# Hybrid decoder step on one core: the attention probabilities are scaled by their sums on the vector engine, head by head, in place of GpSimd

## The chip, the cores and the metric

The kernel runs on 1 core of one Trainium2 chip. The metric is the device time of one execution in microseconds (us); the lower the better. A core has five engines that run their own instruction streams and meet at semaphores: TensorE (PE: matmuls and transposes into the PSUM memory), VectorE (DVE), ScalarE (ACT), GpSimd (POOL) and SyncE (SP, which here only starts DMAs). The profile names a TensorE weight load PEld, and an engine's queue instructions (semaphores, drains, DMA issues) by a q behind its name.

## The reference

Four layers, each `x <- x + RMSNorm_post(mixer(RMSNorm_pre(x)))`, on 1024 prompt tokens and 8 sample tokens, which share all weights. Layer 0 and 3 are gated MLPs, layer 2 is a gated linear recurrence, and layer 1, the one that the change touches, is attention over a sliding window of 128 keys, with a sink value for each of its 16 heads:

```python
def sink_softmax(scores, mask, sinks):
    s = jnp.where(mask, scores.astype(jnp.float32), -jnp.inf)
    sink = sinks.astype(jnp.float32)[..., None, None]
    m = jnp.maximum(jnp.max(s, axis=-1, keepdims=True), sink)
    e = jnp.exp(s - m)
    return e / (jnp.sum(e, axis=-1, keepdims=True) + jnp.exp(sink - m))
...
    o = jnp.einsum('bnkgqs,bnskd->bnqkgd', p.astype(vv.dtype), vv).reshape(bsz, t_len, N_HEADS * HEAD_DIM)
    out = (o * jax.nn.silu(g)) @ w_out
```

What is changed is the division by the sum, for the prompt tokens: the exponentials `e` are multiplied by the reciprocal of their sum.

## The kernel before, in words

Everything is fp32. A matrix product is made of three matmul passes on parts of the operands (high x high, low x high, high x low); the high part of a weight tile is made by ACT (`w_high`, L992), the low part by DVE (`w_low`, L1434), and each weight tile is loaded by SP into a ring of three places. Activations lie with features on the 128 partitions and 1032 tokens along the free dimension, worked on in three parts of 344 columns.

In the attention layer (`layer_b` on each engine) the prompt is cut into 8 blocks of 128 queries, and the 16 heads into 4 groups of 4. That makes 32 steps (`STEPS`), and in step `i` an engine does its part for several steps at once. The chain of one step is

- PE `scores(i)` (L816): queries by keys into PSUM, 4 heads x 256 keys;
- DVE `maxima(i)` (L1773): scale, mask and row maximum, from PSUM to the SBUF tile `sc` (one of two buffers, `i % 2`), 4 operations; it ends with signal `B`;
- ACT `exps(i)` (L1278): the exponentials in place in `sc`, with their sums, 4 operations; ends with signal `X`;
- DVE `sums(i)` (L1784, L1786): sum plus sink, and reciprocal, into `rq`; signal `Rq`;
- POOL `normals` (L527): one operation multiplies `sc`, 128 rows x 4 heads x 256, by `rq`; signal `C`;
- PE `turns(i)` (L830): transposes `sc` (16 of them) into PSUM; signal `TP`;
- ACT `copies(i)` (L1287): PSUM to `pt`; signal `PC`;
- PE `values(i)` (L844): the product with the values; signal `PV`;
- DVE `outputs(i)` (L1794), ACT `highs(i)` (L1294), DVE `lows(i)` (L1800): gate, and split into high and low for the output product.

The order on each engine is written out by hand. In its iteration `i` DVE does `maxima(i + 1)`, then the readings of projection pieces (`read_piece`, L1752 and L1749), `outputs(i - 1)`, `lows(i - 2)`, then `sums(i + 1)`, and behind it what the step brings: `gate_silu` (L1762), `w_low` and `rotate_q` (the rotary turn of a query tile: L1700, L1701, L1703; six times in the steps, the first three earlier) and the pieces of attention for the sample tokens (`sample_keys` L1806 to L1815, `sample_maxima` L1820 to L1828, `sample_normals` L1833 to L1842, `sample_probs`). ACT does `copies(i - 1)`, `exps(i + 1)`, `highs(i - 1)`, and behind them DMA issues of `swap` (L1228, which feeds the rotary turn), `w_high` and `gate_tanh` (L1272). PE does pieces of the query and gate projections (`piece`, L798, 24 matmuls each), `values(i - 1)`, `scores(i + 2)` and `turns(i)`; from step 27 on, pieces of the output product (`out_part`, L855) stand in the place of the projections. `maxima(i + 1)` waits for `scores(i + 1)` and for `turns(i - 1)`, which frees its buffer.

The lines of the attention loop on DVE are these:

```python
for i in range(STEPS):
    if i + 1 < STEPS:
        maxima(i + 1)
    ...
    if i + 1 < STEPS:
        sums(i + 1)
    for p in late_end(i - 1) if i else ():
        gate_silu(p)
    ...
    for j in units_ended(i - 1) if i else []:
        w_low(L.u0 + j + 2)
        ...
            rotate_q(m)
```

Of the kernel before, what the change touches and what calls it, by code (L numbers as in the profile page):

```python
# [17 lines left out]
ALU = mybir.AluOpType  # L18
# [3 lines left out]
P = 128  # L22
# [11 lines left out]
WIN = 128  # L34
# [51 lines left out]
def build(nc, io):  # L86
    with ExitStack() as ctx:
# [76 lines left out]
        for i, kind in enumerate("abca"):  # L164
            L = Layer()
# [49 lines left out]
            if kind == "b":  # L215
# [9 lines left out]
                o = X_AT  # L225
# [37 lines left out]
            if kind == "c":  # L263
# [23 lines left out]
                o = X_AT  # L287
# [85 lines left out]
        STEPS = 4 * NBLK  # L373
# [13 lines left out]
        def pieces_ended(entries):  # L387

            return [p for p, _, end in entries if end == KT]
# [130 lines left out]
        @block.gpsimd  # L520
        def _(pool):

            def normals(L):

                for i in range(STEPS):
                    pool.wait_ge(*L.Rq.at(i + 1))
                    nc.gpsimd.tensor_tensor(L.sc[:, i % 2], L.sc[:, i % 2],  # L527
                                            L.rq[:, i % 2].rearrange("p (h o) -> p h o", o=1).to_broadcast([P, 4, 2 * WIN]),
                                            ALU.mult).then_inc(L.C.sem, 1)

            def gate_input(L, m):

                pool.wait_ge(*L.sig.at(m + 1))
                nc.gpsimd.tensor_tensor(L.it[:, m % 2, :], L.it[:, m % 2, :], L.xc[:, m, :], ALU.mult).then_inc(L.ix.sem, 1)

            LA, LB, LC, LZ = layers
            normals(LB)
            for m in range(KT):
                gate_input(LC, m)

# [880 lines left out]
        def _(dve):  # L1421
            V = nc.vector
# [269 lines left out]
            def layer_b(L):  # L1692
# [88 lines left out]
                def sums(i):  # L1781
                    p = i % 2
                    dve.wait_ge(*L.X.at(i + 1))
                    V.tensor_tensor(L.rq[:, p], L.mx[:, p, 2, :], L.mx[:, p, 3, :], ALU.add)  # L1784
                    V.drain()
                    V.reciprocal(L.rq[:, p], L.rq[:, p]).then_inc(L.Rq.sem, 1)  # L1786

                def outputs(i):
                    qd, n = divmod(i, NBLK)
# [76 lines left out]
                dve.wait_ge(*L.at_in.at(16 * 5))  # L1866
                maxima(0)
                sums(0)
                to_rotate = []
                for i in range(STEPS):  # L1870
# [11 lines left out]
                    if i + 1 < STEPS:  # L1882
                        sums(i + 1)
# [294 lines left out]
```

## Time and profile before

| | before |
|---|---|
| median of 3 runs | 2393.58 us (2392.2 to 2395.04) |
| the profiled execution | 2394.26 us, its span 2392.1 us |
| PE busy | 2320.3 us, 97% of the span |
| DVE busy | 1232.4 us, 52% |
| ACT busy | 889.1 us, 37% |
| POOL busy | 90.7 us, 4% |
| granted TensorE clock, mean | 0.99 of full |
| the attention steps | about 885 to 1145 us of the span |
| PE busy in the attention steps | 241.47 of 260 us |
| DVE, ACT, POOL busy there | 172.47, 138.84, 70.46 us |

Times in rows are microseconds from the start of the span, unless a column says ns. Busy shares tell little by themselves: what counts is which engine the others wait for, stretch by stretch.

### The profile page before, as it was taken

What the parts mean: (1) busy time and instruction counts of PE and PEld (TensorE: products, weight loads), DVE (VectorE), ACT (ScalarE), POOL (GpSimd) and SP (SyncE); (2) the same over time, 40 slices, a digit from 0 to 9 for tenths busy, and PEclk for the clock granted to TensorE, in tenths of its full rate; (3) what the DMA queues carried; (4) which work ended last, traced back from release to release, by engine and by line L of the source; (5) the groups of instructions that cost most, each with busy time, mean ns of one, the idle gap of its engine ahead of it and who ended that gap; (6) DMA issues with size and microseconds to landing.
All of it is one profiled execution on the core that took longest, in us unless ns stands there. A gap on an engine that the chain in (4) does not pass through costs nothing.

```text
span 2392.1 us, 36016 instructions
## 1 busy us (share of the span) xinstructions
PE 2320.3 (97%) x15487; PEld 2236.2 (93%) x15487; DVE 1232.4 (52%) x1759; ACT 889.1 (37%) x1280; POOL 90.7 (4%) x44
## 2 busy tenths in 40 slices
PE   8999999999999899998999999999999999999997
PEld 7999999999999798877989999979999999999996
DVE  4444445454433756667267888274444544545235
ACT  5323332332332534556352366363223332333221
POOL 0000000000000002222000010000000000000000
PEclk9999999999999999999999999999999999999998
DMA  4111111111121331111322111322111111111213
GB/s 137 45 45 45 45 45 38 43 45 45 36 98 45 127 111 54 45 45 37 107 83 70 45 45 45 118 84 77 45 54 36 45 45 38 43 45 45 89 46 107
DMA packets 58494, 145.86 MB, mean 61 GB/s; under 512 B 8904, under 2 KB 29528, under 8 KB 58328
## 3 DMA queue, kind: packets, MB, share of 16 engines
q1 hardware_dynamic: 53056, 135.34, 17.5%
q10 hardware_dynamic: 5280, 8.22, 1.3%
q8 instruction: 122, 2.00, 0.4%
q14 instruction: 36, 0.29, 0.0%
HBM read 121.47 MB, written 18.37 MB: 58 GB/s over the span
## 4 chain that ended last, share of the span: by engine, by line
PE 82%; DVE 9%; ACT 3%; DVEq 3%; ACTq 1%; issue 1%; DMA 1%; SPq 0%
PE ps L552 62%; PE ps L576 7%; PE ps L798 4%; PE ps L710 2%; PE ps L634 2%; DVE x L1476 1%; DVE l_acc L1473 1%; PE ps L816 1%; DVE w_lo L1434 1%; PE ps L855 1%; PE ps L844 1%; PE ps L703 1%; DVE l_sc L1773 1%; ACT l_h_hi L1043 1%; DVE l_hs L1988 1%
## 5 line engine op out<-in xcount | busy, mean ns | idle before, releaser
L552 PE MATMUL ps<-l_h_hi,w_hi 128*128 128x344 f32 x2448 | 527.1, 324 | 5.6 <-DVE w_lo L1434 5.6
L552 PE MATMUL ps<-l_h_lo,w_hi 128*128 128x344 f32 x2448 | 520.4, 321 | 0.0
L552 PE MATMUL ps<-l_h_hi,w_lo 128*128 128x344 f32 x2448 | 516.6, 319 | 0.0
L552 PEld LDWEIGHTS ps<-l_h_hi,w_hi 128*128 128x128 f32 x2448 | 409.2, 188 | 10.1 <-DVE w_lo L1434 6.8
L552 PEld LDWEIGHTS ps<-l_h_lo,w_hi 128*128 128x128 f32 x2448 | 414.7, 189 | 0.0
L552 PEld LDWEIGHTS ps<-l_h_hi,w_lo 128*128 128x128 f32 x2448 | 408.2, 188 | 0.0
L1434 DVE TENSOR_TENSOR w_lo<-w_raw,w_hi 128x1024 fp32r<-128x1024 f32 x182 | 227.7, 1252 | 250.3 <-ACT w_hi L992 240.2
L992 ACT ACTIVATE w_hi<-w_raw 128x1024 fp32r<-128x1024 f32 x182 | 190.8, 1049 | 109.9 <-DMA w_raw<-in_wu 78.9
L1551 DVE TENSOR_TENSOR l_tmp<-ps,rx 128x1032 f32<-128x1032 f32 x64 | 78.9, 1233 | 285.5 <-PE ps L552 285.3
L552 PE MATMUL ps<-l_y_lo,w_hi 128*128 128x344 f32 x816 | 173.1, 320 | 0.0
L552 PE MATMUL ps<-l_y_hi,w_hi 128*128 128x344 f32 x726 | 154.7, 321 | 0.8 <-DVEq L2002 0.8
L552 PE MATMUL ps<-l_y_hi,w_lo 128*128 128x344 f32 x726 | 153.1, 319 | 0.0
L1137 ACT ACTIVATE l_tmp<-l_tmp 128x1032 f32<-128x1032 f32 x32 | 34.2, 1067 | 303.9 <-DVEq L1592 303.9
L552 PEld LDWEIGHTS ps<-l_y_lo,w_hi 128*128 128x128 f32 x816 | 137.9, 189 | 0.0
L552 PEld LDWEIGHTS ps<-l_y_hi,w_hi 128*128 128x128 f32 x726 | 121.6, 188 | 1.7 <-DVEq L2002 1.1
L552 PEld LDWEIGHTS ps<-l_y_hi,w_lo 128*128 128x128 f32 x726 | 120.9, 188 | 0.0
L1142 ACT ACTIVATE l_tmp<-l_tmp 128x1032 f32<-128x1032 f32 x32 | 34.2, 1068 | 226.6 <-DVEq L1597 226.5
L1121 ACT ACTIVATE l_v<-l_v 128x1032 f32<-128x1032 f32 x32 | 34.1, 1067 | 214.9 <-DVEq L1573 214.9
L527 POOL TENSOR_TENSOR l_sc<-l_sc,l_rq 128x1024 f32<-128x1024 f32 x32 | 70.5, 2202 | 1072.6 <-DVE l_rq L1786 1072.6
L798 PE MATMUL ps<-l_h_hi,w_hi 128*128 128x344 f32 x288 | 97.1, 337 | 0.0
L1551 DVE TENSOR_TENSOR l_v<-ps,rx 128x1032 f32<-128x1032 f32 x28 | 34.5, 1233 | 120.2 <-PE ps L552 118.1
L1278 ACT ACTIVATE l_sc<-l_sc,l_mx 128x256 f32<-128x256 f32 x128 | 63.5, 497 | 82.3 <-DVEq L1779 82.3
(248 smaller groups left out, 3617.5 us busy)
## 6 DMA issues: line engine op xcount, KB each, us to landing
w_raw<-in_wu SPq DMA_DIRECT2D x182, 512.0 KB, 3.5
x_save<-x SPq DMA_DIRECT2D x9, 1376.0 KB, 5.8
x<-x_save SPq DMA_DIRECT2D x21, 516.0 KB, 7.1
l_sw<-l_q ACTq DMA_DIRECT2D x32, 129.0 KB, 2.8
out_y<-x SPq DMA_DIRECT2D x6, 688.0 KB, 3.5
x<-in_xt SPq DMA_DIRECT2D x4, 688.0 KB, 10.7
x<-in_xt SPq DMA_DIRECT2D x5, 516.0 KB, 6.7
x<-in_xt ACTq DMA_DIRECT2D x3, 516.0 KB, 3.6
```

The source lines that it names most:

```text
L527: nc.gpsimd.tensor_tensor(L.sc[:, i % 2], L.sc[:, i % 2], L.rq[:, i % 2].rearrange("p (h o) -> p h o", o=1).to_broadcast([P, 4, 2 * WIN]), ...
L552: mm = nc.tensor.matmul(ps[:, 3 * slot + ch, 0:CW], wt[:, w, k, :], mv[:, k, ch * CW:(ch + 1) * CW], start=(k == 0 and t == 0), stop=(k == ...
L576: mm = nc.tensor.matmul(ps[:, 3 * slot + ch, 0:CW], wt[:, u % W_RING, k, :], mv[:, k, part(ch)], start=(k == 0 and t == 0), stop=(k == KT ...
L634: mm = nc.tensor.matmul(ps[:, 3 * j + c, 0:CW], wt[:, (u + j) % W_RING, k, :], mv[:, k, part(c)], start=(k == 0 and t == 0), stop=(k == KT ...
L710: mm = nc.tensor.matmul(ps[:, 6 + b // 4, (b % 4) * P:(b % 4 + 1) * P], vt[:, b, :], L.ws[:, g, :], start=True, stop=True)
L798: mm = nc.tensor.matmul(ps[:, p % 2, 0:CW], wt[:, w % W_RING, k, :], mv[:, k, part(ch)], start=(k == 0 and t == 0), stop=(k == KT - 1 and ...
L992: nc.scalar.activation(w_hi[:, u % W_RING], w_raw[:, u % W_RING], ACT.Copy).then_inc(w_hi_done, 1)
L1137: nc.scalar.activation(L.tmp[:, 0, :], L.tmp[:, 0, :], ACT.Gelu_apprx_tanh).then_inc(L.u_act.sem, 1)
L1142: nc.scalar.activation(L.tmp[:, 1, :], L.tmp[:, 1, :], ACT.Silu).then_inc(L.g_act.sem, 1)
L1278: nc.scalar.activation(L.sc[:, p, h, :], L.sc[:, p, h, :], ACT.Exp, bias=L.mx[:, p, 1, h:h + 1], accum_out=L.mx[:, p, 2, h:h + 1])
L1434: V.tensor_tensor(w_lo[:, u % W_RING], w_raw[:, u % W_RING], w_hi[:, u % W_RING], ALU.subtract).then_inc(w_lo_done, 1)
L1551: V.tensor_tensor(chunks(out), psum_result(slot), chunks(rx[:]), ALU.mult)
```

## The change

The 32 POOL multiplications of `sc` go, with the signal `Rq`. In their place DVE, directly behind the reciprocal, drains and does four `tensor_scalar` operations, one for each head (128 rows x 256 columns, SBUF to SBUF in place, the factor a column of `rq`); the last one gives signal `C`. PE, ACT and SP do what they did. POOL keeps the 8 multiplications of `gate_input` in layer 2.

```diff
         @block.gpsimd
         def _(pool):
-            def normals(L):
-
-                for i in range(STEPS):
-                    pool.wait_ge(*L.Rq.at(i + 1))
-                    nc.gpsimd.tensor_tensor(L.sc[:, i % 2], L.sc[:, i % 2],
-                                            L.rq[:, i % 2].rearrange("p (h o) -> p h o", o=1).to_broadcast([P, 4, 2 * WIN]),
-                                            ALU.mult).then_inc(L.C.sem, 1)
...
             LA, LB, LC, LZ = layers
-            normals(LB)
...
                     V.tensor_tensor(L.rq[:, p], L.mx[:, p, 2, :], L.mx[:, p, 3, :], ALU.add)
                     V.drain()
-                    V.reciprocal(L.rq[:, p], L.rq[:, p]).then_inc(L.Rq.sem, 1)
+                    V.reciprocal(L.rq[:, p], L.rq[:, p])
+                    V.drain()
+                    for h in range(4):
+                        mult = V.tensor_scalar(L.sc[:, p, h, :], L.sc[:, p, h, :], L.rq[:, p, h:h + 1], None, ALU.mult)
+                    mult.then_inc(L.C.sem, 1)
```

Nine lines go ahead of it, so a DVE line of before stands 9 lower in the changed kernel up to the reciprocal (L1786 is L1777 there), and 5 lower behind it (L1794 is L1789).

On DVE the first rotary turn inside the steps stands, before, in this order behind the sums of step 2 (w_lo is the low part of a weight tile, the next three rows are `rotate_q`, ISA rows are the first of the maxima):

```order
L1784 TENSOR_TENSOR l_rq<-l_mx 128x4
L1786 RECIPROCAL l_rq<-l_rq 128x4
L1434 TENSOR_TENSOR w_lo<-w_raw,w_hi 128x1024
L1700 TENSOR_TENSOR l_sw<-l_sw,l_sin 128x1032
L1701 TENSOR_TENSOR l_q<-l_q,l_cos 128x1032
L1703 TENSOR_TENSOR l_q<-l_q,l_sw 128x1032
L1773 ISA l_sc,l_mx<-ps,l_mask,l_sink 128x256
```

The same place in the changed kernel:

```order
L1775 TENSOR_TENSOR l_rq<-l_mx 128x4
L1777 RECIPROCAL l_rq<-l_rq 128x4
L1780 TENSOR_SCALAR l_sc<-l_sc,l_rq 128x256 x4
L1425 TENSOR_TENSOR w_lo<-w_raw,w_hi 128x1024
L1691 TENSOR_TENSOR l_sw<-l_sw,l_sin 128x1032
L1692 TENSOR_TENSOR l_q<-l_q,l_cos 128x1032
L1694 TENSOR_TENSOR l_q<-l_q,l_sw 128x1032
L1764 ISA l_sc,l_mx<-ps,l_mask,l_sink 128x256
```

The four multiplications stand ahead of the weight's low part, of the rotary turn, and of the maxima of the next step. Near the end of the steps, in DVE's iterations 28 and 29, there is nothing but `sample_probs` between a reciprocal and the next maxima. Before, the first of the two:

```order
L1786 RECIPROCAL l_rq<-l_rq 128x4
L1849 COPY l_pts<-ps 128x256
L1850 TENSOR_TENSOR l_zo<-ps,l_dx 8x128
L1773 ISA l_sc,l_mx<-ps,l_mask,l_sink 128x256
L1773 ISA l_mx 128x1
```

And in the changed kernel:

```order
L1777 RECIPROCAL l_rq<-l_rq 128x4
L1780 TENSOR_SCALAR l_sc<-l_sc,l_rq 128x256 x4
L1844 COPY l_pts<-ps 128x256
L1845 TENSOR_TENSOR l_zo<-ps,l_dx 8x128
L1764 ISA l_sc,l_mx<-ps,l_mask,l_sink 128x256
```

Here too the multiplications come between the reciprocal and the next maxima.

## Rows read from the trace of the kernel before

**Rows 1.** Whom PE waited for from 885 to 1147 us: total, times, longest

```profile
PE ps L844 <- ACT l_pt L1287: 10.5, 7, 3.2
PE ps L816 <- DVEq L1779: 7.9, 4, 2.8
```

**Rows 2.** Timeline of PE in the steps: start, duration; in brackets the idle before

```profile
901.14 1.08 PE L844 MATMUL ps<-l_pt,l_vtok 128*64 128x256 f32 x8 [1.50 <-ACT l_pt L1287]
...
912.38 1.13 PE L816 MATMUL ps<-l_kd,l_q 64*128 64x256 f32 x8 [1.53 <-DVEq L1779]
...
1059.13 1.14 PE L816 MATMUL ps<-l_kd,l_q 64*128 64x256 f32 x8 [1.92 <-DVEq L1779]
...
1066.05 1.98 PE L844 MATMUL ps<-l_pt,l_vtok 128*64 128x256 f32 x8 [3.20 <-ACT l_pt L1287]
...
1091.18 1.14 PE L816 MATMUL ps<-l_kd,l_q 64*128 64x256 f32 x8 [2.81 <-DVEq L1779]
...
1120.99 2.08 PE L816 MATMUL ps<-l_kd,l_q 64*128 64x256 f32 x8 [1.67 <-DVEq L1779]
...
1141.66 1.08 PE L844 MATMUL ps<-l_pt,l_vtok 128*64 128x256 f32 x8 [2.61 <-ACT l_pt L1287]
```

**Rows 3.** The POOL multiplication: ns min/median/max, first and last start

```profile
L527 POOL TENSOR_TENSOR l_sc<-l_sc,l_rq x32: 1894/1897/2788, 892.0 to 1140.7; 128x1024 f32<-128x1024 f32 x32
```

**Rows 4.** Timelines of DVE and POOL at the first rotary turn; L1700 as a group

```profile
903.53 1.19 DVE L1434 TENSOR_TENSOR w_lo<-w_raw,w_hi 128x1024 fp32r<-128x1024 f32 x1
904.64 2.92 DVE L1700 TENSOR_TENSOR l_sw<-l_sw,l_sin 128x1032 f32<-128x1032 f32 x1
...
903.69 2.79 POOL L527 TENSOR_TENSOR l_sc<-l_sc,l_rq 128x1024 f32<-128x1024 f32 x1 [4.51 <-DVE l_rq L1786]
...
L1700 DVE TENSOR_TENSOR l_sw<-l_sw,l_sin x9: 1170/2924/2926, 850.2 to 1070.2; 128x1032 f32<-128x1032 f32 x9
```

**Rows 5.** DVE tensor_scalar elsewhere: L1961 and L1962 with two factors, L1777 with constants

```profile
L1961 DVE TENSOR_SCALAR l_xc<-l_xr,cvec x8: 803/806/809, 1278.6 to 1358.0; 128x1024 f32<-128x1024 f32 x8
...
L1962 DVE TENSOR_SCALAR l_xc<-l_st,cvec x8: 281/284/289, 1279.3 to 1358.7; 128x8 f32<-128x8 f32 x8
...
L1777 DVE TENSOR_SCALAR l_mx<-l_mx x32: 169/170/255, 889.0 to 1137.7; 128x4 f32<-128x4 f32 x32
```

**Rows 6.** Other DVE operations in the steps of which some took longer

```profile
L1762 DVE SCALAR_TENSOR_TENSOR l_gate<-l_th,l_gate x6: 484/486/2032, 1085.2 to 1123.5; 128x344 f32<-128x344 f32 x6
...
L1810 DVE COPY l_qz<-l_q x4: 183/185/1593, 1094.2 to 1096.2; 64x32 f32<-64x32 f32 x4
...
L1824 DVE TENSOR_TENSOR l_sm<-l_sm,l_sk x1: 674/674/674, 1109.3 to 1109.3; 128x2 f32<-128x2 f32 x1
...
L1835 DVE TENSOR_TENSOR l_sm<-l_sm x1: 793/793/793, 1116.9 to 1116.9; 128x2 f32<-128x2 f32 x1
```

**Rows 7.** Timelines of ACT and DVE in the last steps

```profile
1105.16 0.51 ACT L1278 ACTIVATE l_sc<-l_sc,l_mx 128x256 f32<-128x256 f32 x1 [1.16 <-DVEq L1779]
...
1112.86 0.51 ACT L1278 ACTIVATE l_sc<-l_sc,l_mx 128x256 f32<-128x256 f32 x1 [3.62 <-DVEq L1779]
...
1116.39 0.42 DVE L1833 TENSOR_REDUCE l_sm<-l_ss 128x2 f32<-128x258 f32 x1 [0.48 <-ACTq L1317]
...
1120.97 0.51 ACT L1278 ACTIVATE l_sc<-l_sc,l_mx 128x256 f32<-128x256 f32 x1 [3.46 <-DVEq L1779]
...
1123.43 0.18 DVE L1786 RECIPROCAL l_rq<-l_rq 128x4 f32<-128x4 f32 x1
...
1126.30 0.51 ACT L1278 ACTIVATE l_sc<-l_sc,l_mx 128x256 f32<-128x256 f32 x1 [1.31 <-DVEq L1779]
...
1135.93 0.48 DVE L1773 CUSTOM_DVE_ANT_0 l_sc<-ps,l_mask,l_sink 128x256 f32<-128x256 f32 x1 [1.55 <-PE ps L830]
...
1138.01 0.51 ACT L1278 ACTIVATE l_sc<-l_sc,l_mx 128x256 f32<-128x256 f32 x1 [1.16 <-DVEq L1779]
```

**Rows 8.** PE busy and granted clock (PEclk) in a stretch after two stalls

```profile
1120.90:1126.70 5.80, 5.71 (x35) 0.52 0.00 0
```

## The prediction

> **What bounds the kernel now.** The page's busy shares come first: TensorE (PE) works 97% of the span, so only what keeps PE waiting can move the time. The windows view puts the 32 attention steps at 885 to 1145 us, with PE busy for 241.47 of 260 us. The list of waits says whom PE waits for there: never for POOL. It waits 10.5 us in 7 places for ACT's copy of the transposed probabilities, and 7.9 us in 4 places for the drain behind DVE's maxima [rows 1]. The timeline says where: twice near 901 to 912, then at 1059, 1066, 1091, 1121 and 1142 [rows 2]. Between 912 and 998 PE goes on without a stall, because pieces of projections fill it, so whatever DVE does there is hidden.
>
> The POOL multiplication takes 1.90 us [rows 3], yet the transposes that need it come a full PE iteration later and never wait. So a shorter way from the reciprocal to the transposes gains nothing by itself. What counts is DVE's own order: reciprocal, then low part and rotary turn, or directly the next maxima, for which ACT's exponentials wait, and behind these PE.
>
> **What the four multiplications cost on DVE.** A tensor_scalar with two factors per row takes 806 ns for 1024 columns and 284 ns for 8 [rows 5], so 0.51 ns a column and 0.28 us fixed. With constants, 4 columns take 0.17 us. For 256 columns that is 0.13 us of columns on 0.17 to 0.28 fixed: 0.30 to 0.41 us. One factor lies between: 0.36. Operations that need not wait for each other start some 0.08 us before the last one ends (L1700 starts at 904.64, while L1434, from 903.53 for 1.19, ends at 904.72 [rows 4]), so four of them take 4 x 0.28 = 1.1 us (0.9 to 1.3). The added drain costs about 0.15 us, since the operation behind the reciprocal no longer starts before that ends. One scaling delays what follows it on DVE by M = 1.25 us, with 1.05 to 1.5 as bounds. All 32 cost DVE 40 us, and DVE has 88 us idle in the steps. The price depends on where they stand.
>
> **What DVE gets back.** The timeline at the first rotary turn shows DVE and POOL in each other's way: POOL's operation from 903.69 took 2.79 us in place of 1.90, and L1700 took 2.92 us [rows 4], though its shortest is 1.17 and L1434 of nearly the same size took 1.19. POOL's operation ends at 906.48; counting from there, L1700 had 1.08 us left, its whole work. So each waits for the other to end. Six of nine rotary turns are in the steps, and the median of the nine is the long time: 1.7 us each comes back. There is more [rows 6]: one gate operation at 2.03 against 0.49 (1.55 back), one copy at 1.59 against 0.18 (1.4), two tiny ones at 0.67 and 0.79, where I take 0.15 as their own time (0.5 and 0.6).
>
> The Trainium skill (SBUF — State Buffer, Who interferes with whom) calls this an exclusive lock, which a DVE operation meets when it has two SBUF inputs and POOL reads SBUF too; by that rule the maxima, with PSUM and one SBUF input, have nothing to get back, and the trace agrees: the first of them at 1135.93 takes 0.48 us under a running POOL operation [rows 7]. This rule speaks for the change, and by it alone, at 1.7 us for six turns on the path, the sum would be up to 10 us faster; the places below say why it isn't.
>
> **The sum, place by place.**
>
> At 901 and 912: step 1's reciprocal is followed directly by maxima, its delay reaches ACT's exponentials, then the four DMA issues and the high part behind them, then the copy for which PE waits at 901.14. That is M less about 0.2 us of slack: +1.0. Then DVE does the next scaling ahead of the rotary turn, which is 1.7 shorter: M - 1.7 = -0.45. PE, at 912.38, is +0.6 late.
>
> At 998 and 1059: each stall is behind a rotary turn. The turn gives 1.7 and takes M: -0.45 both times. At 1059 another scaling stands ahead of maxima that used to wait 0.8 us for PE anyway, and adds 0.4. Tally at 1059 and 1066: about 0.
>
> From 1066 to 1105 PE waits for DVE and ACT in nearly each step. Five scalings cost 6.25; one turn (1.7), the gate operation (1.55) and the copy (1.4) give 4.65; about 0.8 us more falls into time in which DVE waited for PE. Tally at the exponentials of 1105.16: +0.8.
>
> From 1105.16 to 1138.01 [rows 7] the steps are a closed loop on two engines: exponentials, sums, maxima, next exponentials. Those at 1120.97 and 1126.30 are 5.33 us apart: 2.64 to the end of the reciprocal (1123.61), and 2.69 for one gate operation and the maxima. POOL is not in the loop. Five scalings go into it: 6.25 us. Back come 0.5 + 0.6 from the tiny ones. DVE's waits at 1116.39 (0.48, of which 0.4 can be used) and at 1135.93 (1.55) take up 1.95. Net +3.1.
>
> Behind the last exponentials ACT makes the copy for which PE waits at 1141.66; this stall grows from 2.6 to between 3 and 3.5 us. From there PE is full to the end of the layer, so the delay stays. **Sum: +0.8 + 3.1 = +3.9 us.** On the profiled execution's 2394.26 us that is 2398.2; that one lies 0.7 above the median of the three runs, and against the median 2393.58 it is 2397.5. That is 0.16%, and I take 0.2% (4.8 us) as what a measurement can tell from no change.
>
> The last two tallies hold some ten scalings in series, so an error in M of 0.1 moves the sum by 1.0 to 1.5 us; the bounds give about +2 (waits for PE set a floor) and +7.
>
> **Rivals.**
>
> A. The clock. After stalls PE works slower: the scores at 1120.99 took 2.08 us where those at 1059.13 took 1.14, and the copy-fed product at 1066.05 took 1.98 where others take 1.08 [rows 2]; the window behind 1120.9 has a granted clock of 0.52, the lower of the two levels, 1.2 GHz [rows 8]. A stretch like that, 5.8 us long, costs some 2.5 us when nothing else is late. The stall of 2.6 us at 1141.66 had no such stretch behind it; that of 3.2 us at 1066 had. Grown past 3 us it may get one, where PE is the bound; so may the grown pair at 901 and 912. One such stretch adds 1.5 to 2.5 us: +5.4 to +6.4, or 2399 to 2400. Chance 0.25.
>
> B. DVE without its double rate. If the multiplication with one factor ran one column at a time, it would be near the maxima's 0.40 us, and M 1.8: 0.5 more in ten places on top of the sum, +9, or 2403. Against it is the slope, 0.51 ns a column, where L1434 needs 1.19 us for 1024. The Trainium skill (VectorE: DVE Perf Modes, Mode 2×_2P) gives the double rate to a single fp32 source from and to SBUF; the rows of its price agree, hence only a chance of 0.1.
>
> C. Not slower: the locks were on the path more than I count. If the turns ahead of 912, 998, 1059 and 1078 each bring the full 1.7, the gate operation and the copy 3, the tiny ones 1.1, the return is 10.9. With M at its lower bound, and the scalings of the last loop in part beside the gate and sample pieces, perhaps four of them counting on the path (4.2), the kernel would be 6.7 faster, 2387. It is decided in the loop of [rows 7]: only if the time from exponentials to exponentials grows by less than half of M. I see nothing there that a scaling could lie beside, since ACT waits for the maxima in each step (3.62, 3.46, 1.31 and 1.16 us). Chance 0.07.
>
> D. Hidden after all: M is near its lower bound or the middle of the steps gives more back, and the end is +0 to +2, or 2394 to 2395.5. Chance 0.18.
>
> The forecast itself, +2 to +5.4, has 0.4. Its larger part lies within 0.2%. So faster: 0.07. Same: D, and 0.3 of the 0.4, is 0.48. Slower: A, B and the rest, 0.45. The range reaches from the lower end of D to the upper end of A and half-way to B: 2393 to 2402.
>
> **What would show each step.** The new group (DVE tensor_scalar, 128 x 256, x128) should have a mean of 0.36 us; at 0.45 or more B is on. The longest L1700 of the steps (now L1691) should be 1.23 us, and the long ones of [rows 6] should be gone. Exponentials in the last steps should be 6.6 us apart where they were 5.33. PE's stall for the copy at 901 should grow to 2.5, the last one past 3, and the steps should end near 1149 in place of 1145. POOL should be busy for 20 us. A second look goes to the granted clock behind 1145: one more low stretch means A. I am wrong if the distance of exponentials in the last steps stays under 6 us, or if the end of the steps moves by less than 1 or more than 7 us.

## The result and the profile after

| | before | after |
|---|---|---|
| median | 2393.52 us (13 runs, 2389.79 to 2395.04) | 2397.70 us (13 runs, 2396.18 to 2401.26) |
| ratio to before | | 1.0022, 95% interval 1.0014 to 1.0030 |
| profiled execution, span | 2394.26, 2392.1 us | 2401.26, 2399.1 us |
| DVE busy | 1232.4 us | 1252.4 us |
| POOL busy | 90.7 us | 20.3 us |

The kernel became 4.2 us slower by the medians, 0.17%; the ratio in the table isn't that of the medians and comes out at 5.3 us, with an interval of 3.4 to 7.2. 3.9 us and 0.16% were forecast. The profiled execution of after is the slowest of its 13, which matters below. Of the 26 executions of before beside e5 to e8, two ran at a granted clock of 0.61 and 0.56 and took 3490 and 3770 us; no figure below counts them.

First the price of the scaling and of what met POOL before, as groups of after (L1780 is the new scaling; L1691 was L1700, L1753 was L1762, L1805 was L1810, L1830 was L1835):

```profile
L1780 DVE TENSOR_SCALAR l_sc<-l_sc,l_rq x128: 343/348/356, 892.1 to 1148.6; 128x256 f32<-128x256 f32 x128
...
L1691 DVE TENSOR_TENSOR l_sw<-l_sw,l_sin x9: 1169/1226/1236, 850.3 to 1073.8; 128x1032 f32<-128x1032 f32 x9
...
L1753 DVE SCALAR_TENSOR_TENSOR l_gate<-l_th,l_gate x6: 510/512/518, 1089.4 to 1129.7; 128x344 f32<-128x344 f32 x6
...
L1805 DVE COPY l_qz<-l_q x4: 179/182/186, 1098.1 to 1098.7; 64x32 f32<-64x32 f32 x4
...
L1830 DVE TENSOR_TENSOR l_sm<-l_sm x1: 161/161/161, 1122.5 to 1122.5; 128x2 f32<-128x2 f32 x1
```

One multiplication takes 0.35 us, where 0.36 was forecast from [rows 5]. Nothing on DVE is long any more of what was long in [rows 4] and [rows 6]: the rotary operation went from 2.92 to 1.23 us.

Next the last steps of after, on DVE (one scaling) and on ACT (the start of each step's exponentials), the answer to [rows 7]:

```profile
1128.43 0.18 DVE L1777 RECIPROCAL l_rq<-l_rq 128x4 f32<-128x4 f32 x1
1128.68 1.14 DVE L1780 TENSOR_SCALAR l_sc<-l_sc,l_rq 128x256 f32<-128x256 f32 x4
1129.74 0.51 DVE L1753 SCALAR_TENSOR_TENSOR l_gate<-l_th,l_gate 128x344 f32<-128x344 f32 x1
```

```profile
1109.19 0.51 ACT L1269 ACTIVATE l_sc<-l_sc,l_mx 128x256 f32<-128x256 f32 x1 [1.17 <-DVEq L1770]
1117.63 0.51 ACT L1269 ACTIVATE l_sc<-l_sc,l_mx 128x256 f32<-128x256 f32 x1 [4.36 <-DVEq L1770]
1125.97 0.51 ACT L1269 ACTIVATE l_sc<-l_sc,l_mx 128x256 f32<-128x256 f32 x1 [3.69 <-DVEq L1770]
1132.54 0.51 ACT L1269 ACTIVATE l_sc<-l_sc,l_mx 128x256 f32<-128x256 f32 x1 [2.55 <-DVEq L1770]
1139.22 0.51 ACT L1269 ACTIVATE l_sc<-l_sc,l_mx 128x256 f32<-128x256 f32 x1 [3.09 <-DVEq L1770]
1145.07 0.51 ACT L1269 ACTIVATE l_sc<-l_sc,l_mx 128x256 f32<-128x256 f32 x1 [1.30 <-DVEq L1770]
```

From the start of the reciprocal to the next DVE operation is 1.31 us, where before a reciprocal began 0.10 us ahead of the next operation's start (the reciprocal at 1123.43 [rows 7], the gate operation at 1123.53); M, the delay of one scaling, is 1.2 us. The exponentials at 1125.97 and 1132.54 are 6.57 us apart, against 5.33. From the first to the last of these rows there are 35.88 us, against 32.85 before (1105.16 to 1138.01): +3.03, where +3.1 was forecast. But the first row stands at 1109.19, 4.0 us late in place of 0.8.

Not all profiled executions reach the attention steps at the same time, so times from the span's start hold a part that has nothing to do with the scaling. The exponentials of step 0 in before, and in e10, a second profile of the kernel after:

```profile
889.26 0.51 ACT L1278 ACTIVATE l_sc<-l_sc,l_mx 128x256 f32<-128x256 f32 x1 [2.37 <-DVEq L1779]
```

```profile
890.41 0.51 ACT L1269 ACTIVATE l_sc<-l_sc,l_mx 128x256 f32<-128x256 f32 x1 [2.38 <-DVEq L1770]
```

In after they are at 889.38. Counted from these rows, the tally at the first row of the last steps is +3.9 in after and, as e10's row of 1107.45 further down gives, +1.1 in e10.

The timeline of PE says where in after the tally began to grow (start, duration of the eight matmuls, and in the bracket the stall ahead of them):

```profile
902.77 1.98 PE L835 MATMUL ps<-l_pt,l_vtok 128*64 128x256 f32 x8 [3.01 <-ACT l_pt L1278]
...
1061.54 1.13 PE L807 MATMUL ps<-l_kd,l_q 64*128 64x256 f32 x8 [2.08 <-DVEq L1770]
...
1148.72 1.97 PE L835 MATMUL ps<-l_pt,l_vtok 128*64 128x256 f32 x8 [3.18 <-ACT l_pt L1278]
```

and the windows of after behind the last and the first of them (length of the window, then the busy time of PE, of its weight loads, DVE, ACT and POOL, then the granted clock; the last two columns are DMA):

```profile
1147.60:1150.60 3.00, 1.88 (x8) 0.77 (x8) 2.88 (x10) 1.07 (x2) 0.00 (x0) 0.55 0.00 0
901.80:908.40 6.60, 5.63 (x35) 3.93 (x36) 3.46 (x9) 4.14 (x13) 0.00 (x0) 0.52 0.01 3
```

The stall at 901, 1.50 us before, was forecast at 2.5 and became 3.01. Behind it PE ran 6.6 us at about half clock, which it did not in the profiled execution of before. The half microsecond too much is ACT's four DMA issues, 3.14 us in place of 2.44, and that isn't the scaling's doing: e1, which scales nothing, has 3.21 there, and e10, the same kernel as after, 2.84. The row of after:

```profile
897.56 3.14 ACTq L1219 DMA_DIRECT2D l_sw<-l_q  x4
```

The row of before:

```profile
896.63 2.44 ACTq L1228 DMA_DIRECT2D l_sw<-l_q  x4
```

The last stall grew from 2.61 to 3.18, and there too a stretch of low clock followed that was not there before: rival A in part, twice. A third place lies between the two, where after and e10 differ although they are one kernel and the stall is the same 2.54 us. In after the clock was low behind it, in e10 (second row) it was not:

```profile
1093.88 2.08 PE L807 MATMUL ps<-l_kd,l_q 64*128 64x256 f32 x8 [2.54 <-DVEq L1770]
```

```profile
1093.22 1.14 PE L807 MATMUL ps<-l_kd,l_q 64*128 64x256 f32 x8 [2.54 <-DVEq L1770]
```

From 885 to 1150 us the mean granted clock is 0.97 before, 0.94 in after and 0.97 in e10. Behind this third place the exponentials are 7.65 us apart in after (1101.54 to 1109.19) and 6.57 in e10 (1100.88 to 1107.45). So low clock makes part of what the profiled execution of after has above the median, and it isn't needed for the +4: e10 has the mean clock of before and is, at the last stall, 5.3 us later than before (1146.97 against 1141.66), of which 1.15 came ahead of the steps.

### The profile page after: what moved, and what is told of

It reads as the page before. It is cut to its first block, busy times and chain, and to the rows that moved or that the text cites. A ratio compares the mean times of both kernels' runs of the same rounds, so it can differ in the third digit from the quotient of the medians.

```text
span 2399.1 us, 36144 instructions
## 1 busy us (share of the span) xinstructions
PE 2329.2 (97%) x15487; PEld 2242.8 (93%) x15487; DVE 1252.4 (52%) x1887; ACT 889.1 (37%) x1280; POOL 20.3 (1%) x12
## 4 chain that ended last, share of the span: by engine, by line
PE 81%; DVE 10%; ACT 3%; DVEq 2%; ACTq 2%; issue 1%; DMA 0%; SPq 0%
PE ps L543 61%; PE ps L567 7%; PE ps L789 4%; PE ps L701 2%; PE ps L625 2%; DVE x L1467 1%; DVE l_acc L1464 1%; PE ps L835 1%; DVE w_lo L1425 1%; DVE l_sc L1764 1%; PE ps L694 1%; ACTq L1272 1%; PE ps L807 1%; PE ps L846 1%; ACT l_h_hi L1034 1%
## 5 line engine op out<-in xcount | busy, mean ns | idle before, releaser
L543 PE MATMUL ps<-l_h_lo,w_hi 128*128 128x344 f32 x2448 | 520.6, 321 | 0.0
L789 PE MATMUL ps<-l_h_lo,w_hi 128*128 128x344 f32 x288 | 93.3, 324 | 0.0
```

What stands on the lines that cost most here:

```text
L543: mm = nc.tensor.matmul(ps[:, 3 * slot + ch, 0:CW], wt[:, w, k, :], mv[:, k, ch * CW:(ch + 1) * CW], start=(k == 0 and t == 0), stop=(k == ...
L789: mm = nc.tensor.matmul(ps[:, p % 2, 0:CW], wt[:, w % W_RING, k, :], mv[:, k, part(ch)], start=(k == 0 and t == 0), stop=(k == KT - 1 and ...
```

## The experiments

Each was timed in five rounds with the kernel before on the same chip; e1 to e4 stood side by side on one chip, e5 to e8 on a second, e9 to e11 on a third. The table has them all, and "on before" is the difference of medians in us. The interval of a ratio is some 2 to 3 us wide on each side, so differences between rows hold to about 3 us.

| | who scales, where | median us | on before | ratio (95%) |
|---|---|---|---|---|
| after | DVE, behind the reciprocal | 2397.70 | +4.2 | 1.0014 to 1.0030 |
| e1 | nobody | 2384.34 | -7.9 | 0.9950 to 0.9977 |
| e2 | DVE, behind the next maxima | 2385.37 | -6.9 | 0.9955 to 0.9980 |
| e3 | POOL, and DVE by one | 2413.22 | +21.0 | 1.0070 to 1.0098 |
| e4 | DVE, twice | 2419.78 | +27.5 | 1.0097 to 1.0124 |
| e5 | DVE in steps 25 to 31, POOL else | 2397.49 | +5.1 | 1.0015 to 1.0034 |
| e6 | DVE in steps 0 to 24, POOL else | 2395.29 | +2.9 | 1.0002 to 1.0020 |
| e7 | POOL, signalled later | 2386.28 | -6.1 | 0.9965 to 0.9983 |
| e8 | DVE, one operation | 2401.32 | +8.9 | 1.0019 to 1.0044 |
| e9 | DVE, end of its iteration | 2398.79 | +5.0 | 1.0010 to 1.0030 |
| e10 | as after | 2399.03 | +5.3 | 1.0013 to 1.0033 |
| e11 | as e2 | 2385.61 | -8.1 | 0.9958 to 0.9981 |

**e1: nobody scales.** The division by the sum is left out.

```diff
                     V.reciprocal(L.rq[:, p], L.rq[:, p])
-                    V.drain()
-                    for h in range(4):
-                        mult = V.tensor_scalar(L.sc[:, p, h, :], L.sc[:, p, h, :], L.rq[:, p, h:h + 1], None, ALU.mult)
-                    mult.then_inc(L.C.sem, 1)
+                    V.drain().then_inc(L.C.sem, 1)
```

> The kernel of after without the scaling: neither DVE nor POOL multiplies the exponentials (the division by the sum is left out, so the output is not normalised); the reciprocal's drain gives signal C. Theory 1 (DVE's order decides; POOL's lock on DVE was worth 8 to 10 us on the path before, the scaling costs 12 us on it after): 6 to 9 us faster than before, 2385 to 2388. Rival (POOL was hidden with all it did, and the lock too; only the added work counts): within 1 us of before.

Measured: 7.9 us faster than before. So POOL, for whose result PE never waited, cost the kernel before 7.9 us, and the scaling on DVE costs after 12 us (4.2 + 7.9). Ten scalings in series at 1.2 us, as the prediction counted, are also 12 us; the agreement doesn't show the count, since part of each delay falls into slack.

The exponentials at both ends of the last steps, in e1:

```profile
1098.91 0.51 ACT L1269 ACTIVATE l_sc<-l_sc,l_mx 128x256 f32<-128x256 f32 x1 [1.16 <-DVEq L1770]
...
1130.80 0.51 ACT L1269 ACTIVATE l_sc<-l_sc,l_mx 128x256 f32<-128x256 f32 x1 [1.17 <-DVEq L1770]
```

They are 31.89 us apart, 1.0 less than before: that is what left with POOL in the last steps, where the prediction counted 1.1. The rest, 6.4 us counted from step 0, had been gained by 1098.91. The scaling costs 4.0 in the last steps (35.88 against 31.89), where the prediction has 6.25 less 1.95, or 4.3.

**e7: POOL scales, but doesn't meet DVE's wide operations.**

```diff
-                    V.reciprocal(L.rq[:, p], L.rq[:, p]).then_inc(L.Rq.sem, 1)
+                    V.reciprocal(L.rq[:, p], L.rq[:, p])
...
                 sums(0)
+                V.drain().then_inc(L.Rq.sem, 1)
...
                     if i == 30:
                         sample_outputs()
+                    if i + 1 < STEPS:
+                        V.drain().then_inc(L.Rq.sem, 1)
```

> POOL scales as in before, but its signal is given at the end of DVE's iteration, behind the low part, the rotary turn and the other pieces, so that its operation no longer meets them. DVE does no scaling. Theory 1 (the lock alone was worth 8 us): 4 to 8 us faster than before, near e1 and e2. Rival (POOL's later end makes the transposes wait, or the lock was worth nothing): -1 to +3 us.

Measured: 6.1 us faster than before, with the same 32 POOL operations. Their row, and that of the rotary operation, in e7:

```profile
L527 POOL TENSOR_TENSOR l_sc<-l_sc,l_rq x32: 1892/1893/1896, 892.3 to 1135.4; 128x1024 f32<-128x1024 f32 x32
...
L1700 DVE TENSOR_TENSOR l_sw<-l_sw,l_sin x9: 1169/1226/1234, 850.4 to 1066.1; 128x1032 f32<-128x1032 f32 x9
```

No POOL operation takes over 1.90 us, where the longest took 2.79 in [rows 3], and no rotary operation over 1.23. What moved is the time of the signal alone, up to some 5 us later, with a drain at the end of each iteration. So the cost of POOL before was its meeting with DVE's operations, not its length nor the wait for it. PE does wait for POOL once in e7, 0.87 us at 1137.32, which the 6.1 includes.

**e2: the same work on DVE, behind the next step's maxima.**

```diff
                     V.reciprocal(L.rq[:, p], L.rq[:, p])
+
+                def scale(i):
+                    p = i % 2
                     V.drain()
...
                     if i + 1 < STEPS:
                         maxima(i + 1)
+                    scale(i)
```

> The same four multiplications on DVE, but behind the next step's maxima, where DVE has waited for ACT's exponentials. Theory 1: they lie beside the exponentials, the loop of the last steps goes back to about 5.4 us, and what the lock cost stays away: 4 to 8 us faster than before, 2386 to 2390. Rival (the added work on DVE costs wherever it stands): +3 to +5 us, as after.

Measured: 6.9 us faster than before (8.1 in e11, its repetition), 1 us from the kernel that doesn't scale at all, which is within the noise. The chip does the same 128 multiplications on DVE as in after. The timeline of DVE in e2, and the exponentials on ACT in the same steps, show where they lie:

```profile
1118.17 0.15 DVE L1769 TENSOR_TENSOR l_mx<-l_sink,l_mx 128x4 f32<-128x4 f32 x1
1118.50 1.14 DVE L1783 TENSOR_SCALAR l_sc<-l_sc,l_rq 128x256 f32<-128x256 f32 x4 [0.17 <-issue]
1119.55 0.42 DVE L1792 TENSOR_TENSOR l_gate<-ps,l_gate 128x256 f32<-128x256 f32 x1
1119.89 0.41 DVE L1798 TENSOR_TENSOR l_y_lo<-l_gate,l_y_hi 128x256 fp32r<-128x256 f32 x1
1120.61 0.16 DVE L1775 TENSOR_TENSOR l_rq<-l_mx 128x4 f32<-128x4 f32 x1 [0.31 <-ACTq L1272]
```

```profile
1118.39 0.51 ACT L1269 ACTIVATE l_sc<-l_sc,l_mx 128x256 f32<-128x256 f32 x1 [1.79 <-DVEq L1770]
1123.83 0.51 ACT L1269 ACTIVATE l_sc<-l_sc,l_mx 128x256 f32<-128x256 f32 x1 [1.84 <-DVEq L1770]
```

The scaling starts 0.1 us behind the exponentials and fills time in which DVE would wait for them; it still waits 0.31 us before the sums. The loop takes 5.44 us. The chance of such cover, which rival C looked for behind the reciprocal, is not there but one operation group further.

**e9: the scaling behind the rotary turn, but ahead of the maxima.** As e2, with `scale(0)` ahead of the loop and `scale(i + 1)` at the end of DVE's iteration instead:

```diff
                     if i == 30:
                         sample_outputs()
+                    if i + 1 < STEPS:
+                        scale(i + 1)
```

> The four multiplications of after moved to the end of DVE's iteration: behind the weight's low part, the rotary turn, gate and sample pieces, but still ahead of the next maxima. Theory 1 (the maxima are what must not be delayed): no better than after, +3 to +6 us on before. Rival (it is the weight's low part and the rotary turn that must not be delayed): 3 us or more faster than after, near e2.

> The kernel of after once more, unchanged, beside e9 on the same chip: +4 us on before.

Measured: 2398.79 against 2399.03 for after on the same chip, and e2's kernel again (e11) at 2385.61. Whether the scaling precedes the weight's low part and the rotary turn makes no difference beyond the noise. Ahead of the maxima it costs, and behind them it doesn't: e11 is 13.4 us faster than e10 on the same chip, where 10 to 12 was expected.

> The kernel of e2 once more, unchanged, on the same chip: 6 to 8 us faster than before and 10 to 12 faster than after.

**e3: work and lock together.** In the kernel of before, ahead of the reciprocal:

```diff
+                    for h in range(4):
+                        V.tensor_scalar(L.sc[:, p, h, :], L.sc[:, p, h, :], ones[:, 0:1], None, ALU.mult)
+                    V.drain()
                     V.reciprocal(L.rq[:, p], L.rq[:, p]).then_inc(L.Rq.sem, 1)
```

> The kernel of before, with POOL scaling as it did, and on top four multiplications by one on DVE in the same tile, ahead of the reciprocal: work and lock together. Theory 1 (work 12 us, lock 8 to 10 us, about independent): +10 to +14 us on before, 2404 to 2408. Rival (the lock was never on the path): +4 us, as after, 2397 to 2398.

**e4: twice the scaling.** In the kernel of after, behind the four multiplications:

```diff
+                    V.drain()
+                    for h in range(4):
+                        mult = V.tensor_scalar(L.sc[:, p, h, :], L.sc[:, p, h, :], ones[:, 0:1], None, ALU.mult)
                     mult.then_inc(L.C.sem, 1)
```

> The kernel of after with the four multiplications done twice, the second time by one. M grows from 1.2 to 2.4 us. Theory 1 (ten or more scalings in series on the path, with slack used up): 11 to 15 us slower than after, +15 to +19 on before. Rival (only the three of the last loop and one at the start are on the path): +4 to +5 us on after.

Both missed: +21.0 where 10 to 14 was expected, and 23 us on after where 11 to 15 was. With e1 and before they make a square: scaling on DVE alone costs 12.1 (after less e1), on top of the lock 21.0 (e3 less before; POOL's signal is also 1.2 us later there), a second time 23.3 (e4 less after). The first 1.2 us in each of 32 steps cost 0.38 us a step, the next 0.73. The waits of PE in e4, from 885 to 1170 us, show what grew:

```profile
PE ps L807 <- DVEq L1770: 22.6, 15, 3.7
PE ps L835 <- ACT l_pt L1278: 15.0, 8, 4.4
```

PE waits for the maxima in 15 places, 22.6 us in all. In before it was 4 [rows 1], in after 5 with 7.1 us, in e10 8 with 9.0 us. I had taken the number of scalings in series as fixed. It grows, as the slack in the middle steps is used up; the two costs on DVE, of the lock and of the work, are not independent.

**e5 and e6: which steps.** Scaling by DVE in steps 25 to 31 alone (e5), or in steps 0 to 24 alone (e6), and by POOL in the others:

```diff
-                    V.reciprocal(L.rq[:, p], L.rq[:, p]).then_inc(L.Rq.sem, 1)
+                    recip = V.reciprocal(L.rq[:, p], L.rq[:, p])
+                    if not 25 <= i < 32:
+                        recip.then_inc(L.Rq.sem, 1)
+                    else:
+                        V.drain()
+                        if i:
+                            dve.wait_ge(*L.C.at(i))
+                        for h in range(4):
+                            mult = V.tensor_scalar(L.sc[:, p, h, :], L.sc[:, p, h, :], L.rq[:, p, h:h + 1], None, ALU.mult)
+                        mult.then_inc(L.C.sem, 1)
```

> Steps 25 to 31 scaled on DVE as in after, steps 0 to 24 on POOL as in before. If the prediction's second half is right, the loop of the last steps alone gives +3 us on before. Rival (low clock of PE after grown stalls, early in the steps, is what made after slower): +1 us or less.

> Steps 0 to 24 scaled on DVE, steps 25 to 31 on POOL. By the prediction's first half +0.8 us on before. Rival (as the profiled execution of after has it at step 26, with a stretch of low clock at 902): +3 to +4 us.

Measured: +5.1 and +2.9, where +3 and +0.8 were expected. The two together are more than after's +4.2 to +5.3; the intervals, some 2 us each way, leave room for additivity and don't show it. The first and last exponentials of the last steps in e5:

```profile
1104.87 0.51 ACT L1279 ACTIVATE l_sc<-l_sc,l_mx 128x256 f32<-128x256 f32 x1 [2.52 <-DVEq L1780]
1141.09 0.51 ACT L1279 ACTIVATE l_sc<-l_sc,l_mx 128x256 f32<-128x256 f32 x1 [1.30 <-DVEq L1780]
```

And in e6:

```profile
1107.35 0.51 ACT L1279 ACTIVATE l_sc<-l_sc,l_mx 128x256 f32<-128x256 f32 x1 [1.16 <-DVEq L1780]
1140.82 0.51 ACT L1279 ACTIVATE l_sc<-l_sc,l_mx 128x256 f32<-128x256 f32 x1 [1.16 <-DVEq L1780]
```

The last steps take 36.22 us in e5 (+3.4 on the 32.85 of before) and 33.47 in e6 (+0.6). Counted from the exponentials of step 0 (888.90 in e5, 890.16 in e6), the first of the last steps are late by 0.1 in e5 and by 1.3 in e6. So in both profiles the place is as forecast. What the first half is worth, the times don't settle: e6's interval is 0.5 to 4.8 us, which holds the 0.8 and the rival's 3 to 4. e5 also answers for the clock: its mean from 885 to 1150 us is 0.99, above the 0.97 of before, and the last steps still take 3.4 us more.

**e8: one operation in place of four.** In after:

```diff
-                    for h in range(4):
-                        mult = V.tensor_scalar(L.sc[:, p, h, :], L.sc[:, p, h, :], L.rq[:, p, h:h + 1], None, ALU.mult)
+                    mult = V.tensor_tensor(L.sc[:, p], L.sc[:, p], L.rq[:, p].rearrange("p (h o) -> p h o", o=1).to_broadcast([P, 4, 2 * WIN]),
+                                           ALU.mult)
```

> The kernel of after with one tensor_tensor of 1024 columns and a broadcast factor in the place of four tensor_scalar of 256 columns. It should take 1.22 us, 1.14 from start to start of the next, against 4 x 0.26 = 1.06: M grows by 0.1. Theory (only the length on DVE counts): within +0 to +3 us of after, +4 to +7 on before. Rival (the fixed cost of four instructions is what costs): 2 us or more faster than after.

Measured: +8.9, between 0.19% and 0.44%, where +4 to +7 was expected; its operation takes 1.23 us. By difference of medians it is slower than after by 4.7 and than e10 by 3.6, where 0 to 3 was expected, and the intervals overlap. The sign is as expected; the noise doesn't tell whether the size is above it. That the four short operations are the worse choice by 2 us is excluded.

## Why the prediction was right

**What bounds** held: in before PE waited for DVE's maxima and ACT's copy and never for POOL. e1 and e7 show that a shorter way from reciprocal to transposes had no part in it: with a shorter way and with a longer one the kernel gains the same within the noise, once the lock is gone.

**The price** held: 0.35 us for 0.36, M of 1.2 us for 1.25. Rival B is out.

**The return of the lock** held in each row, and on the path it was 7.9 us (e1) or 6.1 (e7). What the prediction had put on the path was 1.7 in four places, 1.55, 1.4 and 1.1, or 10.9 us, less the slack that it fell into.

**The last loop**, +3.1, was 3.03 in after (the prediction's own terms, 6.25 less 1.1 less 1.95, add up to 3.2), and 3.02 in e10 (1107.45 to 1143.32 in its timeline):

```profile
1107.45 0.51 ACT L1269 ACTIVATE l_sc<-l_sc,l_mx 128x256 f32<-128x256 f32 x1 [2.52 <-DVEq L1770]
1143.32 0.51 ACT L1269 ACTIVATE l_sc<-l_sc,l_mx 128x256 f32<-128x256 f32 x1 [1.30 <-DVEq L1770]
```

**The first tally**, "Tally at the exponentials of 1105.16: +0.8", counted from the exponentials of step 0, is 1.1 in e10, 1.3 in e6 and 3.9 in the profiled execution of after. e10, which is nearer to its median, follows the forecast place by place: +1.1 there, +3.0 in the last steps, and the last stall 4.2 us later than before on the same count. The profile of after has more at two places. At the first the stall ended 1.6 us later (902.77 against 901.14) in place of 1.0, because ACT's DMA issues took 0.7 us longer. They took 2.44 to 3.33 us in the 13 profiles, whatever the kernel; why is open. Then came the low clock behind 902 and 1094.

How much of this is luck? The place and the size of the loss in the last steps are not: three profiles (after, e10, e5) have it at 3.0 to 3.4. That the sum of +3.9 lies 0.3 from the median of +4.2 is: after's own interval is 3.4 to 7.2, its repetition measured +5.3, and two profiled executions of one kernel, after and e10, end the steps 2.7 us apart, with the low clock that I had set apart as a rival and not put into the sum. And one sign of being wrong was touched. The prediction names an end of the steps that moves by more than 7 us; in the profile of after the last stall ended 7.06 us later. In e10 it was 5.31, and counted from step 0 the two are 6.9 and 4.2. I read this as the low clock of that execution and not as a fault of the tally, since the same kernel in e10 stays within the bounds.

**Rival A** came true in part: low clock behind the stalls of 3.01 and 3.18 us in after, and of 2.71 and 3.17 us in e10, where before had none. It isn't the cause of the +4, as e5 and the mean clock of e10 show; how much of the median it makes up is open. What A says of the stall's length, none behind 2.6 us and one behind 3.2, doesn't hold as a rule: a stall of 2.54 us had low clock behind it in after and none in e10. **C** is out with the loop: the exponentials grew apart by 1.24 us, more than half of M, and the whole lock was worth less than the whole scaling. **D**, +0 to +2 us, is out: the interval of after begins at 3.4.

The version that beats both kernels is e2: 6.9 and 8.1 us faster than before on two chips, 0.30 to 0.32%, and 13.4 faster than after on the same chip.

## What to carry to other kernels

Ask of work that moves to another engine which operation there stands behind it, and who waits for that one; the same four multiplications cost some 12 us ahead of the maxima and, within the noise, nothing behind them. An engine that nobody waits for can still cost time through operations of another engine that it blocks; look for one line with two durations in the trace. Before reading how late a row is in one profile against another, take off how late the stage began, here up to 1.6 us, and look at a second profile of the same kernel. A cost repeated in each step is worth more per microsecond the more of the slack is used up, so a price taken from a doubled cost, here 0.73 us a step, is not the price of the single one, 0.38.

## What the runs showed of the hardware

The lock is mutual and for the whole operation: the POOL multiplication, SBUF to SBUF, went from 1.90 to 2.79 us when DVE's w_lo (two SBUF inputs) had begun ahead of it. Behind POOL a rotary operation took 2.92 us in place of 1.23 and a gate operation 2.03 in place of 0.49, both with two SBUF inputs; one copy of 64x32 with a single SBUF input took 1.59 in place of 0.18, so two inputs are not the only case. By the Trainium skill (SBUF — State Buffer, Who interferes with whom) the maxima, which read PSUM and one SBUF tile, stay clear. The trace agrees: all 128 of them took 0.47 to 0.49 us, before with POOL at work and in after without it.

PE's granted clock varies between runs of the same program: over the 13 runs of after it was 0.986 to 0.993, with 2401.26 us at the lowest and 2396.18 at the highest. Not each stretch of low clock is paid for, since in the last steps PE waits for DVE anyway: in before the scores at 1120.99 took 2.08 us at low clock, in e6, where POOL scales these steps too, those at 1123.19 took 1.13 at full clock, and the exponentials around them are 5.33 us apart in both. The length of a stall doesn't tell whether low clock follows. Of the stalls in the profiles read here those of 2.27 (e1, at 902.05), 2.71, 3.01, 3.18 and 3.20 us had it behind them, those of 2.61 and of 3.13 (e5, at 1065.88) had not, and that of 2.54 had it in one profile of the kernel and not in the other.
